# Who makes the low part of one weight piece at two layer borders: GpSimd or VectorE

## What is computed

```python
x  = x + mx[2] * rmsnorm(yx, post_norm[l, 0])            # residual
hx = modulate(rmsnorm(x, pre_norm[l, 1]), mx[3], mx[4])  # h*(1+scale)+shift
a, v = jnp.split(hx @ ffn_w_up[l], 2, axis=-1)           # next projection
yx = (silu(conv(a)) * v) @ ffn_w_down[l]
```

## Time and profile before

| | us |
|---|---|
| median of 3 runs (1337.78 to 1338.17) | 1337.94 |
| profiled execution, its own time | 1337.82 |
| its span in the profile | 1336.1 |
| TensorE busy | 1297.3 (97% of the span) |
| VectorE busy | 876.5 (66%) |
| ScalarE busy | 656.1 (49%) |
| GpSimd busy | 334.4 (25%) |

### The profile page before, as it was taken

How to read it: one execution, slowest core, us unless ns; L and a number is a source line. 1 busy time by engine, 2 the same in 40 slices (tenths; PEclk the granted TensorE clock), 3 DMA queues, 4 the chain that set the end, 5 groups by cost and what they waited for, 6 DMA issues and landing times. The chain is left out here.

```text
span 1336.1 us, 22159 instructions
## 1 busy us (share of the span) xinstructions
PE 1297.3 (97%) x8454; PEld 1093.4 (82%) x8454; DVE 876.5 (66%) x1717; ACT 656.1 (49%) x1037; POOL 334.4 (25%) x236
## 2 busy tenths in 40 slices
PE   5999999999999999999999999999999999999997
PEld 2678888887767888888888867899898879899997
DVE  4678777777697644222445778777777877774675
ACT  4445544445356433322333365555555645674664
POOL 1000000000203755105553030210111230683772
PEclk9999999999999999999999999999999999999999
DMA  9643444335470632234324334533333348366753
GB/s 345 202 142 123 131 132 137 127 118 167 158 244 23 190 95 87 71 110 123 98 71 134 103 126 111 158 95 95 95 95 94 95 157 255 110 200 173 219 164 111
DMA packets 274794, 183.28 MB, mean 137 GB/s; under 512 B 6642, under 2 KB 249106, under 8 KB 274706
## 3 DMA queue, kind: packets, MB, share of 16 engines
q1 hardware_dynamic: 274162, 180.00, 44.7%
q10 hardware_dynamic: 544, 2.10, 0.4%
HBM read 181.03 MB, written 1.05 MB: 136 GB/s over the span
## 5 line engine op out<-in xcount | busy, mean ns | idle before, releaser
L2218 PE MATMUL bank<-hh,wh 128*128 128x512 f32 (+1 forms) x1298 | 456.3, 352 | 3.5 <-DVE wl L1394 1.6
L2220 PE MATMUL bank<-hh,wl 128*128 128x512 f32 (+1 forms) x1298 | 451.6, 348 | 0.0
L2219 PE MATMUL bank<-hl,wh 128*128 128x512 f32 (+1 forms) x1298 | 451.2, 348 | 0.0
L849 ACT ACTIVATE wh<-wraw 128x1024 fp32r<-128x1024 f32 (+2 forms) x265 | 256.9, 985 | 84.0 <-PE bank L2220 59.4
L2218 PEld LDWEIGHTS bank<-hh,wh 128*128 128x128 f32 x1298 | 244.0, 188 | 39.1 <-DVE wl L1394 3.5
L1868 DVE SCALAR_TENSOR_TENSOR conv<-bank,pv,conv 128x189 f32<-128x189 f32 (+3 forms) x396 | 172.4, 436 | 152.9 <-ACT conv L1126 138.0
L2220 PEld LDWEIGHTS bank<-hh,wl 128*128 128x128 f32 x1298 | 243.9, 188 | 32.5
L1394 DVE TENSOR_TENSOR wl<-wraw,wh 128x1024 fp32r<-128x1024 f32 (+2 forms) x171 | 192.9, 1149 | 116.9 <-ACT wh L849 116.9
L2219 PEld LDWEIGHTS bank<-hl,wh 128*128 128x128 f32 x1298 | 244.1, 188 | 30.1
L737 POOL TENSOR_TENSOR wl<-wraw,wh 128x1024 fp32r<-128x1024 f32 (+2 forms) x87 | 198.8, 2291 | 197.3 <-ACT wh L849 197.0
L783 POOL TENSOR_TENSOR hl<-yT,hh 128x512 fp32r<-128x512 f32 x13 | 19.5, 1522 | 352.8 <-DVE gates L1764 340.3
(11 more groups left out here) (354 smaller groups left out, 2069.0 us busy)
## 6 DMA issues: line engine op xcount, KB each, us to landing
wraw<-in_ffn_w_up SPq DMA_DIRECT2D x88, 512.0 KB, 3.9
araw<-in_ada_w SPq DMA_DIRECT2D x40, 1024.0 KB, 8.2
wraw<-in_mb_w_in SPq DMA_DIRECT2D x48, 512.0 KB, 4.0
wraw<-in_hg_w_in SPq DMA_DIRECT2D x40, 512.0 KB, 3.9
wraw<-in_ffn_w_down SPq DMA_DIRECT2D x32, 512.0 KB, 4.0
wraw<-in_mb_w_out SPq DMA_DIRECT2D x16, 512.0 KB, 4.8
gates<-in_ada_w SPq DMA_DIRECT2D x5, 1024.0 KB, 9.3
wraw<-in_hg_w_out SPq DMA_DIRECT2D x8, 512.0 KB, 4.2
```

What stands on the lines that cost most here:

```text
L849: act.activation(slot(whp, n, 0, size), wraw[:, n % SLOTS, 0:size], ACT.Copy).then_inc(w_hi, 1)
L2218: pe.matmul(dst, W, hi(k), start=(k == 0), stop=False, **skip)
L2219: pe.matmul(dst, W, lo(k), start=False, stop=False, **skip)
L2220: ins = pe.matmul(dst, L, hi(k), start=False, stop=(k == nk - 1), **skip)
```

## The change

The low parts of the two pieces are made by GpSimd. `part(at["b", 0])` stands in its list after `split_rest(0, T)` and before `norm_low(1, T)`, `part(at["up", 1, 0, 1, 1])` after `y_low(1, ...)` and before `norm_low(2, SEQ)`. VectorE no longer makes them in `add_and_norm`. The engine's name for both pieces is changed in `sub`, so TensorE and SyncE wait for GpSimd's count there.

```diff
@@ plan_ffn_subs
                     sub(("up", l, half, c, part), SUB, P, cols(a["ffn_w_up"][l], 0, KT, part * FF + (f0 + c) * P, P),
-                        ffp[l, half, "up"][0] + 2 * c + part + 1, "dve" if half == 0 and 2 * c + part < 5 - l or by_vector(l, half, c, part) else "pool")
+                        ffp[l, half, "up"][0] + 2 * c + part + 1, "dve" if half == 0 and 2 * c + part < 5 - 2 * l or by_vector(l, half, c, part) else "pool")
@@ pieces of Mamba
-        sub(("b", g), SUB, P, cols(m_in, 0, KT, B0 + g * P, P), ("b", g))
+        sub(("b", g), SUB, P, cols(m_in, 0, KT, B0 + g * P, P), ("b", g), "dve" if g else "pool")
@@ GpSimd
         split_rest(0, T)
+        part(at["b", 0])
         norm_low(1, T)
...
         y_low(1, range(KT))
+        part(at["up", 1, 0, 1, 1])
         norm_low(2, SEQ)
@@ VectorE
-        def add_and_norm(l, s, n, rows, weight=None):
+        def add_and_norm(l, s, n, rows):
...
-                if m == 1 and weight is not None:
-                    split_lo(weight)
...
-        add_and_norm(0, 1, T, LATE + 5, at["b", 0])
+        add_and_norm(0, 1, T, LATE + 5)
...
-        add_and_norm(1, 0, SEQ, LATE + 11, at["up", 1, 0, 1, 1])
+        add_and_norm(1, 0, SEQ, LATE + 11)
```

## The result

The changed kernel takes 1341.08 us (median of 11 executions) against 1337.99 us before (11, same chip): ratio 1.0022, interval 1.0014 to 1.0029, so 3.1 us slower. The forecast was 1340.3 with a range from 1337.9 to 1342.8. The likeliest of its three cases, "within 0.2%" with 0.60, did not come: 3.1 us is 0.23%. "Slower by over 0.2%" had been given 0.38. The executions do not agree as those of the kernel before do (1337.59 to 1338.41). Five lie at 1339.85 to 1340.36, three at 1341.08 to 1341.39, three at 1342.21 to 1342.25.

A forecast was written before the change was run, and what follows sets the result against it. TensorE, the busiest engine, bounds the kernel, and delays at the two borders fall on it. Border A +1.63 and border B +0.76 on 1337.82 gave 1340.21 for the profiled execution, 1340.3 as median; range 1337.9 to 1342.8 us.

The forecast's parts named there:

- its three cases: Whole kernel's time: slower by over 0.2% (chance 0.38), within 0.2% (0.60), faster by over 0.2% (0.02).
- VectorE's addition stands behind GpSimd in border A: Border A, `variance`: line 1483 stands until GpSimd's subtraction ends, ending at 779.53 instead of 777.65, 1.88 us late.
- Line 1485 in border B: Border B, `variance`: this one-input instruction stands behind GpSimd until 1138.32, so ScalarE's root starts 1.96 us late.
- The rival without it: Border B: line 1485 does not stand still, a pure gain of 1.20 us, sum 1338.4; chance 0.13.
- The chain follows directly: Both borders: `variance`, root, tile 0, then TensorE take the delay in full; TensorE's first wait about 2.3 us.
- The gains: Removing VectorE's low part from the borders saves 0.25 us in A and 1.20 us in B.
- The clock: Rival: TensorE's clock falls after the longer idle time, costing 1.62 us in border A, 0.8 in B; chance 0.27.
- The sum: Whole kernel: border A +1.63 us and border B +0.76 us, giving 1340.3 against 1337.94, 0.18% slower.
- this order: Border B: VectorE's line 1483 starts 0.03 us ahead and GpSimd stands; 1.96 us late, against 2.2 with GpSimd first.

The follow-up runs named there:

- the fill: Changed kernel, but in border A GpSimd twice fills the piece's low part with zeros instead of subtracting; 1339.24 us, one execution.
- B alone: Kernel before, but in border B GpSimd makes the low part, after `variance` has ended; 1336.58 us, ratio 0.9992.
- with 2.45 us in the kernel before: Kernel before with 9 instead of 18 covering matmuls at border A, nothing else changed; 1338.08 us, ratio 1.0002.
- the run with the wait: Changed kernel, but GpSimd also waits for the end of `variance` before each of the two low parts; 1336.62 us, ratio 0.9990.
- border A alone: Changed kernel with border B's half undone, so only border A has GpSimd's low part; 1340.86 us, ratio 1.0021; a later single execution 1341.14 us.

## Why the prediction was right

- *VectorE's addition stands behind GpSimd in border A.* Right in kind and size: forecast 776.96 to 779.53, measured 777.09 to 779.62, with 0.13 us that the profiles are apart. The run with the addition read from PSUM, and the run with GpSimd's part after `variance`, show that the overlap makes the loss. The Trainium skill ("SBUF — State Buffer", section "Who interferes with whom") says that a VectorE instruction with two SBUF inputs contends with a GpSimd instruction that reads SBUF and not with one that only writes it. The traces agree: 2.53 us beside the subtraction, 0.69 beside the fill.
- *Line 1485 in border B.* Forecast at about 2.4 us; measured 2.40. No row of before showed that it would stand: it was inferred from its speed. The rival without it was wrong.
- *"The chain follows directly".* This step was off by a few tenths. The maximum came 1.83 and 2.11 us late, TensorE only 1.67 and 1.61, and it waited 2.07 and 2.04 us for its first tile where 2.3 was forecast. The root was not on the path before: in A its result was in PSUM at 779.50, while the multiplication that needs it (line 1526) started at 779.85, directly behind line 1513. What comes first behind the maximum is VectorE's own product for tile 0 (line 1496), and that waited for ScalarE's copy of the `ada` rows, which ended at 778.06 in A and 1136.49 in B. In B it stood still for 0.43 us for that; VectorE's timeline before, then after, where the copy is long done:

```profile
1136.60 0.43 DVE L1496 TENSOR_TENSOR bank<-yT,bank 128x256 f32<-128x256 f32 x1 [0.43 <-ACT asum L925]
```

```profile
1139.76 0.42 DVE L1498 TENSOR_TENSOR bank<-yT,bank 128x256 f32<-128x256 f32 x1
```

  This slack, some 0.1 us in A and 0.5 in B, takes that part of the delay. With gains close to the forecast, border A costs 1.42 (forecast 1.63) and border B 0.42 (0.76).
- *The gains.* 0.25 and 1.20 were forecast. With the overlap away, the profile shows 0.27 in A and 1.21 in B. The times show 1.2 us for both and 1.1 for B alone: B's gain is there too, A's is too small for them.
- *The clock.* This was the rival with 0.27, at 1.62 us for a fall in A and 0.8 in B, and it was not in the sum. Its mechanism and prices were right where they could be read: 1.59 us in A and 0.62 in B. By the groups of the times it came in six or more of the eleven executions and made the median's loss 3.1 us instead of the 1.9 to 2.4 of the quick ones. That is what put the result on the far side of 0.2%.
- *The sum.* It had a loss of 2.4 us, with two errors that partly cancel: the delay at the borders was taken about 0.5 us too large (the quickest execution is 1.86 us slower), and the falls of the clock, 1.2 us more for the median, were left out. That 1341.1 lies so near 1340.3 is partly luck.

Open: why, with 2.1 us idle in border A, 8 of 11 executions are over 1 us longer than the other three, and with 2.45 us in the kernel before only 4 of 11 are longer than any of its reference. The clock was seen in one execution of the 8 kind and in none of the 4, of which one is a mere 0.03 us beyond its reference. What TensorE did ahead of the idle time differs (18 covering matmuls or 9, behind the same ones on a quarter of the columns), and so does the place of the gap; neither was tried apart. The earlier load that the change sets free was not tried apart either; the run with the wait keeps it for the most part and is the fastest, so it does no visible harm.

## What to carry to other kernels

Before work moves to an idle GpSimd, look at what VectorE runs in those very microseconds: in these traces an addition with two SBUF inputs, and a fast one-input maximum from SBUF to SBUF, stood still for the rest of GpSimd's subtraction. If VectorE's are on the path to the end, let GpSimd wait a moment: here one wait for each part, which starts it 1.9 us later in border A and 0.8 us later in border B and still in time, turned 3.1 us lost into 1.2 us won. And a cover of spare matmuls fits one length of idle time only: when the gap behind it grew, the median loss was 3.1 us with the old cover and 2.1 with the longer one.

## What the runs showed of the hardware that was not expected

A GpSimd fill of SBUF, which reads nothing, holds VectorE's one-input maximum (1.09 instead of 0.43 us) but not the two-input addition (0.69). In border A GpSimd was ahead of the addition by 0.40 us, and the addition stood still; in border B the addition was ahead by 0.04 us, and GpSimd and then the maximum stood still (2.67 and 2.40 us). The forecast reckoned 1.96 us of delay for this order and 2.2 for the other, so the order should hardly matter; no run had the other one in border B. And 2.1 us of idle time were enough for TensorE's clock to be lowered for a few us in two of the profiled executions (0.54 and 0.64 on the mean of 3 us), while in three others with 2.04 to 2.11 us idle in one or both borders it stayed at 1.00; the two profiled executions with border A alone both waited 2.11 us, and one of them kept its clock: such a loss shows in the spread of the times, and a profile may fall on an execution without it.
